# Both feed-forwards of a decoder trunk in two phases, the norm gains moved from the weights to the inputs, loops unrolled

## What is computed

```python
def rms_norm(x, g, eps=NORM_EPS):
    xf = x.astype(jnp.float32)
    y = xf * lax.rsqrt(jnp.mean(xf * xf, axis=-1, keepdims=True) + eps)
    return (y * g.astype(jnp.float32)).astype(x.dtype)

def swiglu(x, w_gu, w_down):
    g, u = jnp.split(x @ w_gu, 2, axis=-1)
    return (jax.nn.silu(g) * u) @ w_down
...
        f = swiglu(rms_norm(h, ffn1_pre_g[i]), ffn1_w_gu[i], ffn1_w_down[i])
        h = h + 0.5 * rms_norm(f, ffn1_post_g[i])
        u = rms_norm(h, mix_pre_g[i])
...
        h = h + rms_norm(merged @ w_out[i], mix_post_g[i])
        f = swiglu(rms_norm(h, ffn2_pre_g[i]), ffn2_w_gu[i], ffn2_w_down[i])
        h = h + 0.5 * rms_norm(f, ffn2_post_g[i])
        gate = jax.nn.sigmoid(rms_norm(h, ple_pre_g[i]) @ w_ple_gate[i])
        e = (p[i] @ w_ple_proj[i]) * gate
        h = h + rms_norm(e, ple_post_g[i])
```

## Time and profile before

| | before |
|---|---|
| median of three runs, us | 1173.98 (1173.94 to 1174.22) |
| span of the profiled execution, us | 1172.6 |
| that execution's own time, us | not given apart; median less span is 1.4 |
| PE busy | 1164.0 us, 99% |
| PEld busy | 983.8 us, 84% |
| DVE busy | 850.0 us, 72% |
| ACT busy | 721.0 us, 61% |
| POOL busy | 53.0 us, 5% |
| data moved by DMA | 215.37 MB, 184 GB/s in the mean |

### The profile page before, as it was taken

The page is one execution under the profiler, slowest core; times in us unless marked ns, Lnnn a source line. Parts: engine busy times, 40 slices in busy tenths (PEclk is TensorE's granted clock), DMA queues, the critical chain, the costliest instruction groups (busy, mean ns, idle before and its releaser), DMA issues.

```text
span 1172.6 us, 17196 instructions
## 1 busy us (share of the span) xinstructions
PE 1164.0 (99%) x6031; PEld 983.8 (84%) x6031; DVE 850.0 (72%) x1290; ACT 721.0 (61%) x1166; POOL 53.0 (5%) x124
## 2 busy tenths in 40 slices
PE   9999999999999999999999999999999999999997
PEld 7888888888888888888888888888888888888886
DVE  6766776977857776676787776678776677677666
ACT  7555556577755755555685655565776566565555
POOL 4000000000000000000100000010000010000002
PEclk9999999999999999999999999999999999999999
DMA  9656564654354555655556565746434446546550
GB/s 296 217 181 212 171 215 164 226 172 152 121 201 146 191 204 185 208 174 211 179 171 198 172 211 179 240 165 198 171 111 179 162 162 215 194 170 209 179 196 37
DMA packets 138655, 215.37 MB, mean 184 GB/s; under 512 B 6958, under 2 KB 97904, under 8 KB 138608
## 3 DMA queue, kind: packets, MB, share of 16 engines
q1 hardware_dynamic: 135808, 208.43, 52.6%
q10 hardware_dynamic: 2576, 6.29, 1.6%
q0 software_dynamic: 224, 0.04, 0.0%
HBM read 213.68 MB, written 1.05 MB: 183 GB/s over the span
## 4 chain that ended last, share of the span: by engine, by line
PE 99%; DMA 0%; DVE 0%; ACT 0%; issue 0%; POOL 0%; POOLq 0%; DVEq 0%; ACTq 0%
PE ps L1673 23%; PE ps L1546 19%; PE ps L1548 18%; PE ps L1547 18%; PE ps L1683 12%; PE ps L1916 3%; PE ps L1593 1%; PE ps L1925 1%; PE ps L1802 1%; PE ps L1817 1%; PE ps L1776 0%; PE ps L1788 0%; DMA raw<-in_w_ple_proj 0%; PE ps L1831 0%; PE ps L1838 0%; PE ps L1803 0%
## 5 line engine op out<-in xcount | busy, mean ns | idle before, releaser
L1106 DVE SCALAR_TENSOR_TENSOR w_lo<-raw,g_layer,w_hi 128x512 fp32r<-128x512 f32 (+1 forms) x504 | 356.3, 767 | 139.2 <-ACT w_hi L644 139.2
L644 ACT ACTIVATE w_hi<-raw,g_layer 128x512 fp32r<-128x512 f32 (+1 forms) x524 | 346.7, 732 | 113.6 <-PE ps L1683 97.0
L1673 PE MATMUL ps<-x_both,w_hi 128*128 128x512 f32 x1152 | 287.7, 392 | 0.0
L1673 PEld LDWEIGHTS ps<-x_both,w_hi 128*128 128x128 f32 x1152 | 209.3, 189 | 39.4 <-issue 0.4
L1546 PE MATMUL ps<-w_hi,x_both 128*128 128x512 f32 x576 | 231.6, 402 | 0.0
L1548 PE MATMUL ps<-w_hi,x_both 128*128 128x512 f32 x576 | 225.0, 391 | 0.0
L1547 PE MATMUL ps<-w_lo,x_both 128*128 128x512 f32 x576 | 224.4, 390 | 0.0
L1103 DVE TENSOR_TENSOR w_lo<-raw,w_hi 128x1024 fp32r<-128x1024 f32 x114 | 134.8, 1221 | 61.3 <-ACT w_hi L641 61.3
L641 ACT ACTIVATE w_hi<-raw 128x1024 fp32r<-128x1024 f32 x114 | 114.7, 1053 | 92.7 <-PE ps L1548 92.5
L1683 PEld LDWEIGHTS ps<-x_both,w_lo 128*128 128x128 f32 x1152 | 152.6, 191 | 8.4
L1683 PE MATMUL ps<-x_both,w_lo 128*128 128x256 f32 x1152 | 156.0, 283 | 0.0
(11 more groups left out here) (230 smaller groups left out, 1041.7 us busy)
## 6 DMA issues: line engine op xcount, KB each, us to landing
raw<-in_ffn_w_gu SPq DMA_DIRECT2D x170, 512.0 KB, 4.6
raw<-in_ffn_w_down SPq DMA_DIRECT2D x88, 512.0 KB, 4.0
raw<-in_w_in SPq DMA_DIRECT2D x80, 512.0 KB, 4.5
raw<-in_w_out SPq DMA_DIRECT2D x16, 512.0 KB, 4.1
raw<-in_w_ple_gate SPq DMA_DIRECT2D x16, 512.0 KB, 4.1
raw<-in_w_branch_sb SPq DMA_DIRECT2D x8, 512.0 KB, 4.1
raw<-in_w_branch_diff SPq DMA_DIRECT2D x8, 512.0 KB, 4.2
raw<-in_ffn_w_gu SPq DMA_DIRECT2D x12, 256.0 KB, 7.8
```

Of the source, the lines that this page charges most:

```text
L644: last = act.activation(w_hi[:, s, part], raw[:, s, part], ACT.Copy, scale=g_layer[:, g:g + 1])
L1106: last = dve.scalar_tensor_tensor(out=w_lo[:, s, part], in0=raw[:, s, part], scalar=g_layer[:, g:g + 1], in1=whi[:, part], op0=ALU.mult, o ...
L1673: mm = pe.matmul(dst, w_hi[:, s, cols], x_both[:, :, 4 * half + k, :], start=half == 0 and k == 0, stop=stop and k == 3, skip_group_check= ...
```

## The change

- **Two phases.** All gate/up units of a feed-forward come first (22 units), then the eleven down units. The split hidden values of all eleven steps stay on chip in a new tensor (`h_turned`, viewed as `ht`), whose room is that of the attention's tensors. SP, ACT, DVE and PE all follow this order.
- **Step 10 is flat too**, and the transposes of `turn_last_ht` are gone. Since no down sums stand in PSUM in phase one, the flat sums have two sets of four banks, used in turn.
- **Gains go to x.** The weight units carry no gain any more: `high` and `low` take two operations of 1024 per unit for every unit. Instead `high_inputs` and `low_inputs` multiply the gain in for q = 0, 1, 3 and 4. Each 128x128 block of x has its own gain, so a part takes four operations of 128 columns on ACT and four on DVE where it took one of 512 on each. The semaphore still counts once per part, at the last of the four. The gain of the attention's own norm goes the same way, in operations that stay whole (1024 columns).
- **No loops**: all steps are written out.
- **Start.** The host lays out the gains with the channel on the partition, and `p` transposed. The PE transposes of both, the copies of the gains on DVE and `start_layer` are gone; ACT and DVE wait for the gains' DMA before part 1 of x. The 16 warm-up transposes are 17.

The diff, cut to its core:

```diff
 MEANS = 20
-HTS = NC + 1
-HT_TURNS = 3
-FLAT = NC - 2
+G_SUB = 4 * KD
+G_ALL = G_SUB + 1
+G_FIRST = {0: 0, 1: KD, 3: 2 * KD, 4: 3 * KD}
+FLAT = NC - 1
...
+        h_turned = sb("h_turned", [P, NC * HT_SIZE], F32R)
...
-        FLAT_BANK = (6, 7, 4, 5)
-        FIRST_HT_BANK, R_BANK = 2, 3
-        flat_g, flat_u = ([ps[:, b:b + 2, n * SEQ:(n + 1) * SEQ] for n in range(2)] for b in FLAT_BANK[::2])
+        FLAT_BANK = ((6, 7, 4, 5), (0, 1, 2, 3))
+        FIRST_HT_BANK, R_BANK = 6, 7
+
+        def flat_pair(b):
+            return [ps[:, b:b + 2, n * SEQ:(n + 1) * SEQ] for n in range(2)]
+
+        def flat_sums(c, which):
+            return flat_pair(FLAT_BANK[c % 2][2 * which])
...
             def load_ffn(i, u0, w_gu, w_down):
-                if (i, u0) != (0, U_FFN1):
+                for c in range(NC):
                     for s in range(2):
-                        load_gu(i, u0 + s, w_gu, 0, s)
-                    load_gu(i, u0 + 2, w_gu, 1, 0)
-                load_gu(i, u0 + 3, w_gu, 1, 1)
-                load_deep(i, u0 + 4, w_down, 0)
-                with sp_.Fori(2, NC) as c:
-                    load_gu(i, u0 - 1, w_gu, c, 0, c)
-                    load_gu(i, u0, w_gu, c, 1, c)
-                    load_deep(i, u0 + 1, w_down, c * FC - FC, c)
-                load_deep(i, u0 + U_FFN - 1, w_down, (NC - 1) * FC)
+                        if (i, u0) != (0, U_FFN1) or 2 * c + s >= PIECED - 1:
+                            load_gu(i, u0 + 2 * c + s, w_gu, c, s)
+                for c in range(NC):
+                    load_deep(i, u0 + 2 * NC + c, w_down, c * FC)
 
...
-                    pieces = 2 if ks == 4 and gain is not None else 1
-                    n = UNIT // 2 // pieces
-                    for k in range(pieces * half, pieces * half + pieces):
-                        part = slice(k * n, (k + 1) * n)
-                        if gain is None:
-                            last = act.activation(w_hi[:, s, part], raw[:, s, part], ACT.Copy)
-                        else:
-                            g = gain + (k if ks > 1 else 0)
-                            last = act.activation(w_hi[:, s, part], raw[:, s, part], ACT.Copy,
-                                                  scale=g_layer[:, g:g + 1])
-                    last.then_inc(hi_ready, 1)
+                    part = slice(half * UNIT // 2, (half + 1) * UNIT // 2)
+                    act.activation(w_hi[:, s, part], raw[:, s, part], ACT.Copy).then_inc(hi_ready, 1)
...
+                    src, toks = x_bank(i, q, idx).rearrange("p (k n) -> p k n", k=4), slice(t * P, (t + 1) * P)
+                    if q == 2:
+                        last = act.activation(x_hi[:, 4 * n:4 * n + 4, toks], src, ACT.Copy)
+                    else:
+                        for k in range(4):
+                            last = act.activation(x_hi[:, 4 * n + k, toks], src[:, k, :], ACT.Copy,
+                                                  scale=gain_col(i, G_FIRST[q] + 4 * n + k))
+                    last.then_inc(x_high, 1)
...
-                high(i, u0 + 3, g0 + 4, halves=(0,))
+                high(i, u0 + 3, halves=(0,))
                 act.wait_ge(pre_scale, 8 * i + 4 * f + 2)
                 silu(i, f, 0, u0 + 1, 1)
-                high(i, u0 + 3, g0 + 4, halves=(1,))
-                high(i, u0 + 4)
-                keep_r(i, 2 * f)
-                high_first_ht(i, f)
-                high(i, u0 + 5, g0)
-                flat_glu(i, f, 1, u0)
-                high(i, u0 + 6, g0 + 4)
-                with act.Fori(2, NC - 1) as c:
-                    high(i, u0 + 1, c=c)
-                    high_ht(i, f, c - 1)
-                    high(i, u0 + 2, g0, c=c)
+                high(i, u0 + 3, halves=(1,))
+                for c in range(1, NC):
+                    high(i, u0 + 2 * c + 2)
+                    if c == 1:
+                        keep_r(i, 2 * f)
+                        high_first_ht(i, f)
+                    else:
+                        high_ht(i, f, c - 1)
+                    high(i, u0 + 2 * c + 3)
                     flat_glu(i, f, c, u0)
-                    high(i, u0 + 3, g0 + 4, c=c)
+                high(i, u0 + 2 * NC + 2)
+                high_ht(i, f, NC - 1)
                 loads()
-                high(i, u0 + 3 * NC - 2)
-                high_ht(i, f, NC - 2)
-                high(i, u0 + 3 * NC - 1)
-                silu(i, f, NC - 1, u0 + 3 * NC - 3, 0)
-                act.wait_ge(ht_split, 2 * HTS * i + HTS * f + NC - 1)
-                silu(i, f, NC - 1, u0 + 3 * NC - 3, 1)
-                high_last_ht(i, f, 0)
+                for d in range(3, NC):
+                    high(i, u0 + 2 * NC + d)
                 next_unit()
-                high_last_ht(i, f, 1)
 
             def stick(i, slot_):
 
...
+                    src = x_bank(i, q, idx).rearrange("p (k n) -> p k n", k=4)
+                    if q == 2:
+                        last = dve.tensor_tensor(x_lo[part], src, x_hi[part].bitcast(F32), ALU.subtract)
+                    else:
+                        for k in range(4):
+                            part = (slice(None), 4 * n + k, slice(t * P, (t + 1) * P))
+                            last = dve.scalar_tensor_tensor(out=x_lo[part], in0=src[:, k, :],
+                                                            scalar=gain_col(i, G_FIRST[q] + 4 * n + k),
+                                                            in1=x_hi[part].bitcast(F32), op0=ALU.mult,
+                                                            op1=ALU.subtract)
...
+                def banks_free(step, n):
+
+                    before = 4 * NC * i + 2 * NC * f
+                    if step == 1:
+                        if n and f == 0:
+                            pe.wait_ge(e_kept[1], i + 1)
+                    elif step == 2:
+                        if n == 0:
+                            pe.wait_ge(r_kept, nth_r(i, 2 * f))
+                            pe.wait_ge(ht_split, 2 * NC * i + NC * f + 1)
+                        pe.wait_ge(prod_done, before + 2)
+                    else:
+                        pe.wait_ge(prod_done, before + 2 * (step - 2) + n + 1)
+
...
+                def down(d):
+                    u = u0 + 2 * NC + d
+                    begin(i, u)
+                    pe.wait_ge(ht_split, 2 * NC * i + NC * f + d + 1)
+                    if d == 0:
+                        pe.wait_ge(prod_done, 4 * NC * i + 2 * NC * f + 2 * (NC - 1))
...
-                gate_up(u0 + 3 * NC - 4, 0, NC - 1)
-                gate_up(u0 + 3 * NC - 3, 1, NC - 1)
-                before_last()
-                by_tiles(i, u0 + 3 * NC - 2, last_down, f_done, {
-                    (0, 0): {2: lambda: turn_last_ht(i, f, 0)}, (1, 0): {2: lambda: turn_last_ht(i, f, 1)},
-                    (1, 1): turned_at(i, NEXT_INPUT[q], (0, 1), (1, 2))})
+                for c in range(1, NC):
+                    flat_gate_up(u0 + 2 * c, 0, c)
+                    if c == 1:
+                        if f == 0:
+                            pe.wait_ge(e_kept[0], i + 1)
+                        turn_first_ht(i, f)
+                    flat_gate_up(u0 + 2 * c + 1, 1, c)
+                for d in range(NC - 2):
+                    down(d)
+                by_tiles(i, u0 + 3 * NC - 2, last_down, f_done, {(1, 1): turned_at(i, NEXT_INPUT[q], (0, 1), (1, 2))})
```

More of the change, by code:

```diff
@@ L626, in _, with high @@
             act.preload_act_table_set("silu_and_others")
-            def high(i, u, gain=None, ks=4, c=0, halves=(0, 1)):
+            def high(i, u, c=0, halves=(0, 1)):
                 s = slot(u)
@@ L1118, in low_quarter @@
                     dve.wait_ge(hi_ready, 2 * UNITS * i + 2 * u + k // 2 + 1)
[L1119 to L1122 removed]
+                ins = dve.tensor_tensor(w_lo[:, s, part], raw[:, s, part], w_hi[:, s, part].bitcast(F32), ALU.subtract)
                 if k == 2:
```

443 lines of the change are left out of this document (152 added, 291 removed).

## The result

| | before | after |
|---|---|---|
| median of five runs, us | 1173.97 (1173.79 to 1174.22) | 1193.01 (1192.11 to 1193.76) |
| profiled execution: span, own time, us | 1172.6, own time not given | 1192.0, 1193.76 |
| ratio, 95% interval | | 1.016 (1.0148 to 1.0173) |

The change costs 19.0 us, 1.6%. The sign was forecast; the size (+8.1, at most +14.5) was not. Three lines of the page of the changed kernel: busy times, and the chain that ended last, by engine and by line.

The account below looks back on a forecast made before the run. The prediction took PE's work plus its few waits as the bound (busy 1164.0 of 1172.6 us). Boundaries +9.2 and PE's own work -1.1 gave +8.1: 1182.1 us, range 1175.2 to 1188.5 to hold 8 in 10.

Parts of the forecast that it names:

- PE's own work: Flat step 10 adds 1.1 us; dropped transposes of h and p save 1.8 and 0.4: -1.1 in total.
- boundary to the mixer: Before each mixer, four small operations per part of x lengthen chains that PE waits for: +1.2 us each, two of them.
- to the second feed-forward: Same longer chains for x at the two boundaries to the second feed-forward: +1.2 us each.
- to the gate projection: At these two boundaries parts 1 and 3 of x are needed first, 2 and 4 later: +0.8 us each.
- between the layers: Parts 3 and 4 of x cost 1.0, part 1's operations delaying the first gate/up unit's second half 0.7: +1.7 us.
- operations on x at the start: Parts 2 and 4 cost 1.0, part 3 holds a unit's last quarter by 0.45, less dropped gain copies: +1.1 us.
- Phase one: Gate/up units: ACT, DVE and DMA keep up with PE's 5.58 us per unit; down phase also covered: no cost.
- The dropped gain copies give a bit less back: At the start, removing the gain copies returns slightly less than part 3's 0.45 us delay on DVE.
- absorb the small operations: Rival: at boundaries four operations on x cost no extra time, leaving only PE's saving: 1172.9 us; chance 0.12.
- The loops cost nothing: Denies a rival: 32 loop branches of 0.208 us on PE's queue were paid, so removing them gives 1175.4; chance 0.05.
- Phase one did not starve: Denies a rival: gate/up transfers at 160 GB/s make units 6.55 us, +78 us, 1260 in all; chance 0.03.
- That nothing overlaps: Rival: at boundaries the four operations on x run without overlap, 1.48 us on ACT, 1.36 on DVE: 1195.2; chance 0.05.

Follow-up runs that it names:

- m1: Changed kernel, gains kept on x, with h_turned and os_hi padded to distance 0 from w_hi and the positions' loads behind the gains': 1183.63 us.
- k2: g2 with the positions' two loads issued behind the gains' load, near 8 us: 1172.19 us, ratio 0.9987.
- g2: a2 with other paddings, so that h_turned and os_hi lie at distance 0 modulo 256 from w_hi: 1174.10 us, ratio 1.0001.
- a1: Changed kernel with 32 bytes of padding ahead of the attention tensors and h_turned, and 32 behind: 1187.74 us, ratio 1.0117.
- a2: a1 with the norm gains back in the weight units and one operation per part of x: 1176.42 us, ratio 1.0023.
- j1: Kernel before with its four loops written out and nothing else changed: 1174.31 us, ratio 1.0002.
- f1: Changed kernel, gains in weights, one operation per part of x, each of h_turned's eleven steps laid 32 bytes further than the last: 1178.95 us in one execution.
- c1: Changed kernel, gains in weights, one operation per part of x, every tensor of 512 bytes or more on a multiple of 128: 1179.91 us, ratio 1.0051.

## Why the prediction was wrong, step by step

m1 and k2 differ only in where the gains are multiplied, and k2 and the kernel before differ in the rest. So the starts of the transposes in their timelines split the 19.0 us:

| term | predicted | measured | between |
|---|---|---|---|
| PE's own work | -1.1 | -1.1 | k2 and before, from the start's last transposes to the last gate boundary's: 1128.49 for 1129.59 |
| boundary to the mixer | 1.2 each | 1.3, 1.3 | m1 and k2 |
| to the second feed-forward | 1.2 each | 1.5, 1.3 | m1 and k2 |
| to the gate projection | 0.8 each | 0.9, 0.9 | m1 and k2 |
| between the layers | 1.7 | 1.8 | m1 and k2 |
| operations on x at the start | 1.1 | 2.1 | m1 and k2 |
| host-laid start otherwise | 0 | -0.8 | k2 and before, -1.9 in all, less PE's own -1.1 |
| place of `h_turned`, `os_hi`, `os_lo` | no term | 7.6 | after and m1, same stretch: 1145.83 for 1138.25; 0.65 of it in the two mixers |
| the positions' load | no term | 1.9 | g2 and k2, medians |

Together 18.9 before rounding, for 19.0 measured; the rows mix stretches of single traces with medians, so a tenth or two is not to be had.

**The step that failed** is the assumption under "Phase one" and "What would show it", that the down units stay 5.44 us long. The prediction says "I cost all of this at nothing", and its reasons are about DMA, ACT and DVE alone: it took a product's spacing as a property of its shape. `h_turned`'s room was named in the change, but its address was never asked for. Every down product then cost 0.2333 us instead of 0.2267, 7.0 us in four phases, and the text's own test, "the down units 5.44", failed at once: 5.60.

**The start** was the second miss. "The dropped gain copies give a bit less back" looked at DVE and PE, not at what the removed loads leave on POOL's queue: with one gain load in place of five, the positions' loads come at 2.5 us instead of 4.5, and moving them to 8 us cures the dip. The term of the operations on x at the start was low too: 2.1 for 1.1. The traces of m1 and k2 show it in three pieces, 0.9 before the third transposes, 0.6 before the fourth and 0.6 behind them; the prediction had 1.0, 0.45, and a bit off for the dropped gain copies. The rest of the start gave back 0.8 where the prediction had nothing, and this hides most of that miss in the total.

**Right**: PE's own work to 0.1 in sum, with some luck. Between k2 and before, by the same starts of the last transposes of each boundary, the feed-forward stretches give back 0.4, 0.7, 0.3 and 0.2, 1.6 where 1.1 was forecast, and the two mixer stretches cost 0.3 and 0.2, where nothing was forecast; no run separates the two. Right by their mechanism too: phase one (flat steps start 11.15 us apart, the products of L1598 at 43.06 and 54.21, for 11.16); the operations on x, 1.15 and 1.13 for 1.18 and 1.13, the chain 0.63 + 1.15 + 0.03 + 1.13 = 2.94 for 2.98, 0.48 uncovered for 0.5. A boundary is still 0.1 to 0.3 dearer than forecast; of that h, 0.3 late instead of 0.2, is seen in the traces, the rest is not traced further.

**The rivals.** The boundaries do not absorb the small operations (a1 to a2, 11.3 us). The Trainium skill's "VectorE: DVE Perf Modes", section on the TRN2 errata, gave 1.0 for each four and so 1177.5; m1's trace has 1.15 and 1.13, and its time is 1183.63. Its advice against many small tiles, which it gives for operations that read SBUF, is borne out here on ACT too, which reads the sums from PSUM: 1.15 for four where one took 0.60. The loops cost nothing (j1: 1174.31 against 1174.09). The Trainium skill's "Runtime: NRT & Kernel Launch", Instruction fetch mechanics, speaks of a taken branch whose target is not in the window fetched already; no run here shows such a stall. Phase one did not starve (11.15 us a step). That nothing overlaps (1195.2) came nearest to the number, by luck, and is wrong as a cause: four operations took 1.15, not 1.48.

## What to carry to other kernels

When a tensor moves or grows, look up where its operands land, and compare the spacing of products before and after, not their busy time: a constant extra on each shows in no wait. Whatever is taken off a queue moves the rest of it forward, and a tiny transfer may then fall among the important ones. Work split into small operations is paid where a chain has no slack, and can be priced well from one chain's rows.

## What the runs showed of the hardware

A product of 512 columns (operands declared `F32R`, which the profile writes as f32) with a new 128x128 standing operand starts every 226.7 ns when both operands' addresses in a partition are equal modulo 256, and at other distances:

| standing less moving, mod 256 | 0 | 32 | 64 | 96 | 128 | 160 | 192 | 224 |
|---|---|---|---|---|---|---|---|---|
| ns, f1's first phase | 227.1 | 233.3 | 233.3 | 233.3 | 233.3 | 233.8 | 229.6 | 232.9 |

The values of this table are good to 0.4 ns. Over ten down units other kernels gave 226.7 at 0, 232.4 at 128 (c1), 233.3 at 160 (after) and 228.9 at 192 (a1). The Trainium skill's "SBUF — State Buffer", Operand start alignment, asks only for a multiple of the element size and says that this is about legality, not speed; all these layouts are legal, and of those tried none but distance 0 is free. Why the distance counts is open: no run looks inside the reads. Other shapes were not tried; the flat products, whose operands all lie at distance 0, never changed.

The positions are 256 numbers in two loads of 0.5 KB each. Issued at about 2 us they came with 84 to 197 GB/s between 7 and 8 us in twelve kernels; issued at 8 us, with 265 to 320 in three. At 4.5 us, behind five gain loads, in the kernel before and its four variants, they came with 256 to 325. The kernel before was not run with them early. How they hold the rest up was not tried.
